# Ten chained stages on one core: the 96 conditioning pieces leave the first mixer, their sums and biases move to later chunks

## The chip, the cores and the metric

The kernel runs on one core of a Trainium2 chip. The metric is the device time in microseconds of one execution; lower is better. Each figure is a median of several runs, and one further execution was recorded by the hardware profiler. In what follows TensorE is also PE, VectorE DVE, ScalarE ACT, GpSimd POOL, and SyncE SP.

## The reference, cut to what matters

One sequence of 512 tokens with 1024 channels goes through two models in turn. The first has two layers, each a feed-forward block, a mixer and a second feed-forward block, with RMS norms; the second has two layers, each a hybrid mixer and a convolutional feed-forward block. Before each part of the second model a vector that depends only on the condition c scales and shifts the activations:

```python
cond = jax.nn.silu(c)
for l in range(DEPTH):
    mod = cond @ w_ada[l] + b_ada[l]                 # 1024 -> 6 * 1024, for each of two layers
    sh1, sc1, g1, sh2, sc2, g2 = [m[:, None, :] for m in jnp.split(mod, 6, axis=-1)]
    h = x * (1 + sc1) + sh1
    y = hybrid_mixer(h, ...)
    x = layer_norm(DN_ALPHA * x + g1 * y, ...)
    ...
```

So `mod` is twelve vectors of 1024 numbers (six for each layer). They are first needed when the second model starts; the kernel computes them meanwhile, in the shadow of the first model. This product is what the change moves.

## The kernel before, in words

**Stages and chunks.** All weights stream through the core once. They are cut into 522 chunks of eight 128x128 blocks (512 KB each). The ten stages use them in order: FFN1 (chunks 0 to 65), MIX0, the first mixer (66 to 95), FFN2 (96 to 161), FFN3 (162 to 227), MIX1 (228 to 259), FFN4, then the two hybrid mixers and the two convolutional blocks. `BASE` (L124) holds the first chunk of each stage. A chunk is loaded by SP into one of four RAW buffers, ACT copies its upper part to SPH (`halve_to`, L1541), and DVE makes the remainder SPL (`halve_to`, L2165 to L2177); PE then multiplies each block three times (L806 to L808: high with high, high with low, low with high). ACT and DVE work up to four chunks ahead of PE.

**Conditioning pieces.** Each of the 96 pieces `wa` (512 KB) takes a RAW buffer of its own, one after every two chunks, from chunk 2 to chunk 192. DVE adds c times the piece to ADA (`ada`, L2149 and L2152). Eight pieces make one of the twelve vectors. After the eighth, DVE transposes ADA (L2160) and reduces it to ADS (L2162, event `adas`). PE finishes the sum with eight tiny matmuls `adamm` at the start of a chunk c with c % 16 == 14 (`begin_chunk`, L782 to L790, event `adamm`), which is two chunks ahead of the place of the eighth piece in the order of the chunks. DVE adds the bias (`mods`, L2132 to L2136) when it comes to the first piece of the next vector (L2146 and L2147). The last piece comes with chunk 192.

**PSUM banks.** There are eight banks. Before anything is emitted, a planner walks through the program in PE's order and gives each result a bank (`Ring`, L158 to L184). Without a group it takes the next bank in turn; `ps.before(name)` is then the event after which that bank's former result has been read, and PE waits for it in front of the first matmul. `plan_chunk(c)` (L524 to L526) gives the `adamm` of chunk c a bank in the same turn. `plan_first` plans the six output tiles that the start of a stage (`project_first`) fills at once, then calls `plan_chunk` for the chunks of that stretch, and the stage then takes a bank for its sum of squares (`xsum`). The seventh tile, `("proj", s, 6)`, is planned after that. In a feed-forward stage DVE reads tile 0 as `gate` (L2294), tile 1 as `up` (L2297); in MIX1 it reads the tiles as `qk` (L2546), and there a small product `rcolp` (L1266) follows tile 6.

**The first mixer.** Its projection runs over 22 tiles (`project`, three matmuls for each of eight blocks), and DVE and ACT prepare what the recurrence needs in `prep(j, q)`, at the tiles listed in `PREP_AT`. DVE reads each tile with L2386 or L2389. PE takes part with small products: L1008 and L1010, L1014 (`kqmm`, which waits for ACT's `kq`, L1703), and L1023. Behind the projection an order written out by hand (`MIX0_TENSOR`, `MIX0_VECTOR`, ...) sets the queue of each engine. In it each product of the mixer names its banks by number, so the first of them in a bank waits for whatever tile the planner's turn has left there; the first is `("01", "lt", 1)`. The first four output tiles stand in banks 7, 5, 3 and 2. The remaining four go in turn again (`plan_out`). DVE copies output tile m out of its bank at L2229 (event `("y", s, m)`), after a square by ACT (L1602, L1605).

Of the kernel before, what the change touches and what calls it, by code (L numbers as in the profile page):

```python
# [17 lines left out]
NRAW = 4  # L18
NSPL = 4
ADA_EVERY = 3  # L20
N_ADA = 96
# [99 lines left out]
FFN1, MIX0, FFN2, FFN3, MIX1, FFN4, HYB0, CONV0, HYB1, CONV1 = range(10)  # L121
NAMES = {FFN1: "l0_ffn1", FFN2: "l0_ffn2", FFN3: "l1_ffn1", FFN4: "l1_ffn2"}
CHUNKS = [66, 30, 66, 66, 32, 66, 32, 66, 32, 66]
BASE = [sum(CHUNKS[:s]) for s in range(10)]  # L124
# [181 lines left out]
def build(nc, a, order, known):  # L306

    ctx = ExitStack()
    with ctx:
# [19 lines left out]
        RAW, _ = place("RAW", NRAW * CH * 128)  # L329
# [55 lines left out]
        def pc(name, i=0, n=1):  # L385
            return PCT[:, PC[name] + i:PC[name] + i + n]

        def xt(k):
            return X[:, k * T:(k + 1) * T]
# [13 lines left out]
        IDENT, MEANM, BD = CST[:, 0:128], CST[:, 128:256], CST[:, 256:384]  # L403
        ONE, EPS6, EPS5, EPSG, DECAY = [SML[:, i:i + 1] for i in range(5)]

        def item_of(n):

            return n + min(n // 2, N_ADA)

        def item_of_ada(i):  # L410
            return 3 * i + 2

# [106 lines left out]
        ps = Ring([b for b in banks])  # L521
        scr = Ring([SCR[:, i * T:(i + 1) * T] for i in range(5)])

        def plan_chunk(c):  # L524
            if c % 16 == 14 and c < 2 * N_ADA:
                ps.plan(("adamm", c // 16), ("mod", c // 16))  # L526

        def plan_first(s, name, ended, n=6):
            for i in range(n):
# [248 lines left out]
        def tensor_program(e):  # L778
            w = Waits(e, handles, known)
            tile = [0]  # L780

            def begin_chunk(c):  # L782
                w.wait_ge(("lo", c))
                if c % 16 == 14 and c < 2 * N_ADA:
                    b = c // 16
                    w.wait_ge(("adas", b), ("sel",), *ps.before("adamm", b))
                    for q in range(4):
                        mm = e.matmul(ps["adamm", b][32 * q:32 * q + 32, 0:8], SEL[:], ADS[:, q:32:4], start=True,
                                      stop=True, skip_group_check=True)
                    mm.then_inc(pe_done.did(("adamm", b)))  # L790
# [1337 lines left out]
        def vector_program(e):  # L2128
            w = Waits(e, handles, known)
            halved = [0]  # L2130

            def mods(b):  # L2132
                l, o = b // 6, b % 6
                w.wait_ge(("adamm", b))
                e.tensor_tensor(MOD[:, b * 8:b * 8 + 8], ps["adamm", b][:, 0:8], pc(f"b_ada_2{l}", 8 * o, 8),
                                ALU.add).then_inc(dve_done.did(("mod", b)))  # L2136

            def ada(i):

                b, k = i // 8, i % 8  # L2140
                c = pc("c_2", k)
                r = item_of_ada(i) % NRAW * 1024
                raw = RAW[:, r:r + 1024]
                w.wait_ge(("raw", item_of_ada(i)))
                if k == 0:
                    if b:  # L2146
                        mods(b - 1)  # L2147
                    w.wait_ge(("cond",))
                    e.tensor_scalar(ADA[:], raw, c, None, ALU.mult).then_inc(dve_done.did(("ada", i)))  # L2149
                else:  # L2150
                    w.wait_ge(("ada", i - 1))
                    e.scalar_tensor_tensor(ADA[:], raw, c, ADA[:], ALU.mult, ALU.add).then_inc(  # L2152
                        dve_done.did(("ada", i)))
                if i == 6:
                    w.wait_ge(("cst",))
                    e.tensor_reduce(SEL[:], IDENT.rearrange("p (a r) -> p r a", a=4), AX, ALU.add).then_inc(
                        dve_done.did(("sel",)))
                if k == 7:
                    w.wait_ge(("ada", i))
                    e.transpose(raw, ADA[:]).then_inc(dve_done.did(("adat", b)))  # L2160
                    w.wait_ge(("adat", b), *([("adamm", b - 1)] if b else []))
                    e.tensor_reduce(ADS[:], raw.rearrange("p (b c) -> p b c", c=32), AX, ALU.add).then_inc(  # L2162
                        dve_done.did(("adas", b)))

            def halve_to(c):  # L2165

                while halved[0] <= min(c, a["chunks"] - 1):
                    n = halved[0]
                    if n % 2 == 0 and 0 < n <= 2 * N_ADA:
                        ada(n // 2 - 1)  # L2170
                    if n == 2 * N_ADA + 2:
                        mods(N_ADA // 8 - 1)
                    w.wait_ge(("hi", n))
                    q, r = n % NSPL * 1024, item_of(n) % NRAW * 1024
                    e.tensor_tensor(SPL[:, q:q + 1024], RAW[:, r:r + 1024], SPH[:, q:q + 1024].bitcast(F32),  # L2175
                                    ALU.subtract).then_inc(lo_ready.did(("lo", n)))
                    halved[0] += 1  # L2177
# [906 lines left out]

        def sync_program(e):
            w = Waits(e, handles, known)
            items = [0]

            def load_to(j):

                while items[0] <= j:
                    i = items[0]
                    is_ada = i % 3 == 2 and i // 3 < N_ADA
                    n = i // 3 if is_ada else i - min((i + 1) // 3, N_ADA)
                    items[0] += 1
                    if not is_ada and n >= a["chunks"]:
                        continue
                    if i >= NRAW:
                        f = i - NRAW
                        if f % 3 == 2 and f // 3 < N_ADA:  # L3100
                            w.wait_ge(("adas", f // 24) if f // 3 % 8 == 7 else ("ada", f // 3))
                        else:
                            w.wait_ge(("lo", f - min((f + 1) // 3, N_ADA)))
                    r = i % NRAW
                    e.dma_start(RAW[:, r * 1024:(r + 1) * 1024], a["wa"][n] if is_ada else a["ws"][n]).then_inc(
                        landing(raw_landed[r], ("raw", i)), 16)

            def ahead(s):

                load_to(item_of(BASE[s] + AHEAD) + NRAW - 1)  # L3110

            e.dma_start(PCT[:], a["pc"]).then_inc(landing(pc_landed, ("pc",)), 16)
            for k in range(8):
                e.dma_start(xt(k), a["x"][:, k * T:(k + 1) * T]).then_inc(landing(x_landed[k], ("x", 0, k)), 16)
                if k < 3:
                    load_to(k)
            e.dma_start(CST[:], consts(["ident", "mean", "bd"])).then_inc(landing(cst_landed, ("cst",)), 16)
            for s in range(a["last"] + 1):
                if s == MIX0:
                    ahead(s)  # L3120
                    w.wait_ge(*ah_free(s))
                    e.dma_start(wk(41, 3), a["sm1"]).then_inc(landing(table_landed, ("sm1",)), 16)
                    w.wait_ge(("sm1",))
                    e.dma_start(rwkv["LV"], consts(["incl", "strict", "block", "first", "join2", "join4", "join8", "join16", "diag"])).then_inc(
                        landing(table_landed, ("lv",)), 16)
                elif s == MIX1:
                    ahead(s)
                    w.wait_ge(*ah_free(s), ("lv",))
                    e.dma_start(wk(24)[:, 0:384], consts(["suffix", "ones", "later"])).then_inc(
                        landing(table_landed, ("sufl",)), 16)  # L3130
                elif s in (HYB0, HYB1):
                    ahead(s)
                    H = hyb_places(s)
                    w.wait_ge(*ah_free(s), ("sufl",) if s == HYB0 else ("tables2", HYB0))
                    e.dma_start(WK[:, 23 * T:23 * T + NSM2], a["sm2"][(s - HYB0) // 2]).then_inc(
                        landing(table_landed, ("sm2", s)), 16)
                    w.wait_ge(("sm2", s))
                    e.dma_start(H["C1"][:, 0:3328], consts(["perm", "causal", "cos", "sin", "dec0", "dec1", "dec2",
                                                            "dec3"])).then_inc(
                        landing(table_landed, ("tables1", s)), 16)  # L3140
                    w.wait_ge(("tables1", s))
                    e.dma_start(H["C1"][:, 3328:3584], consts(["cmpm", "cmpn"])).then_inc(
                        landing(table_landed, ("tables2", s)), 16)
            load_to(a["chunks"] + N_ADA - 1)
            for k in range(8):
                w.wait_ge(("x", a["last"] + 1, k))
                e.dma_start(a["out"][:, k * T:(k + 1) * T], xt(k)).then_inc(landing(out_landed, ("out_dma", k)), 16)
            w.wait_ge(("out_dma", 7))
# [141 lines left out]
```

## Time and profile before

| | us |
|---|---|
| median of 3 runs (lowest, highest) | 3435.99 (3434.78, 3438.05) |
| the profiled execution, its own time | 3433.62 |
| its span, from first to last instruction | 3431.9 |
| PE busy (share of the span) | 3349.1 (98%) |
| PE weight loads busy | 2701.2 (79%) |
| DVE busy | 1980.5 (58%) |
| ACT busy | 1354.4 (39%) |
| mean granted clock of PE, as a share of full speed | 0.993 |

Busy times are sums of the records; matmuls overlap in them, so a busy PE isn't PE at its peak. A wait that is put down to a line means that the engine sat idle in front of an instruction until that line's instruction had ended.

### The profile page before, as it was taken

The page shows a single profiled execution, that of the slowest core. Times are in us where ns is not written, and L with a number is a line of the kernel's source. Part 1 is how long each engine was busy: PE and PEld are TensorE (multiplying, and loading weights), DVE is VectorE, ACT ScalarE, POOL GpSimd, SP SyncE. Part 2 cuts the span into 40 slices and gives each one's busy share as a digit, 9 for nine tenths or more (in the row PEclk, how much of TensorE's full clock was granted, in tenths as well). Part 3 has the DMA queues.
Part 4 walks back from the last instruction along what each step waited for, and adds up shares of the span by engine and source line. Part 5 has one row for each costly group of instructions (what it writes and reads, how often), then busy time and mean ns, then how long its engine had stood idle before and what let it go on. Part 6 is the DMA issues. An engine that isn't in the chain of part 4 may idle for free.

```text
span 3431.9 us, 43947 instructions
## 1 busy us (share of the span) xinstructions
PE 3349.1 (98%) x18588; PEld 2701.2 (79%) x18588; DVE 1980.5 (58%) x2869; ACT 1354.4 (39%) x2048; POOL 30.2 (1%) x68
## 2 busy tenths in 40 slices
PE   8999999999999999999999999999999999999998
PEld 6888868788888888886688888757888877578887
DVE  6554687675546653435464435586665365766644
ACT  4332466443324332326443323364443233644433
POOL 0000003000000000000000000000000000000000
PEclk9999999999999999999999999999999999999999
DMA  5444330244443433230122334101322241023231
GB/s 191 146 147 145 127 117 3 89 134 147 146 143 117 161 109 99 89 99 31 38 93 98 99 98 147 56 32 57 103 98 98 80 147 62 14 80 98 94 103 56
DMA packets 93076, 342.28 MB, mean 100 GB/s; under 512 B 10320, under 2 KB 10832, under 8 KB 92368
## 3 DMA queue, kind: packets, MB, share of 16 engines
q1 hardware_dynamic: 92880, 339.48, 30.3%
q8 instruction: 146, 2.39, 0.3%
q14 instruction: 50, 0.41, 0.0%
HBM read 337.34 MB, written 2.10 MB: 99 GB/s over the span
## 4 chain that ended last, share of the span: by engine, by line
PE 86%; DVE 7%; ACT 5%; issue 1%; POOL 0%; DMA 0%; SPq 0%; DVEq 0%; ACTq 0%; POOLq 0%
PE ps L806 21%; PE ps L808 20%; PE ps L807 20%; PE ps L874 3%; PE ps L875 3%; PE ps L878 2%; PE ps L921 1%; PE ps L923 1%; PE ps L922 1%; ACT WK L2069 1%; DVE SPL L2175 1%; PE ps L1296 1%; PE ps L897 1%; PE ps L898 1%; PE ps L899 1%; ACT SPH L1541 1%
## 5 line engine op out<-in xcount | busy, mean ns | idle before, releaser
L2175 DVE TENSOR_TENSOR SPL<-RAW,SPH 128x1024 fp32r<-128x1024 f32 x522 | 635.8, 1224 | 933.2 <-ACT SPH L1541 933.1
L1541 ACT ACTIVATE SPH<-RAW 128x1024 fp32r<-128x1024 f32 x522 | 547.9, 1056 | 976.6 <-PE ps L808 869.8
L806 PE MATMUL ps<-HH,SPH 128*128 128x512 f32 x2328 | 920.2, 395 | 9.2 <-DVE SCR L2294 4.6
L808 PE MATMUL ps<-HH,SPL 128*128 128x512 f32 x2328 | 908.6, 390 | 0.0
L807 PE MATMUL ps<-HL,SPH 128*128 128x512 f32 x2328 | 908.6, 390 | 0.0
L806 PEld LDWEIGHTS ps<-HH,SPH 128*128 128x128 f32 x2328 | 438.1, 188 | 113.5 <-issue 11.1
L807 PEld LDWEIGHTS ps<-HL,SPH 128*128 128x128 f32 x2328 | 438.1, 188 | 94.0 <-issue 4.3
L808 PEld LDWEIGHTS ps<-HH,SPL 128*128 128x128 f32 x2328 | 438.0, 188 | 91.4
L806 PE MATMUL ps<-AH,SPH 128*128 128x512 f32 x996 | 389.4, 391 | 2.7 <-DVE AH L2524 2.7
L808 PE MATMUL ps<-AH,SPL 128*128 128x512 f32 x996 | 388.0, 390 | 0.0
L807 PE MATMUL ps<-AL,SPH 128*128 128x512 f32 x924 | 360.0, 390 | 0.0
L806 PEld LDWEIGHTS ps<-AH,SPH 128*128 128x128 f32 x996 | 187.0, 188 | 43.0 <-DVE AH L2524 3.1
L808 PEld LDWEIGHTS ps<-AH,SPL 128*128 128x128 f32 x996 | 187.0, 188 | 38.9
L807 PEld LDWEIGHTS ps<-AL,SPH 128*128 128x128 f32 x924 | 173.5, 188 | 36.2 <-issue 0.5
L874 PE MATMUL ps<-HH,SPH 128*128 128x512 f32 x390 | 154.1, 395 | 10.7 <-DVE SPL L2175 10.2
L875 PE MATMUL ps<-HH,SPL 128*128 128x512 f32 x390 | 153.5, 394 | 0.0
L1676 ACT ACTIVATE SCR<-SCR 128x512 f32<-128x512 f32 x88 | 55.7, 633 | 170.8 <-DVE SCR L2294 170.8
L2152 DVE SCALAR_TENSOR_TENSOR ADA<-RAW,PCT,ADA 128x1024 f32<-128x1024 f32 x84 | 107.4, 1279 | 0.0
L878 PE MATMUL ps<-HL,SPH 128*128 128x512 f32 x408 | 104.4, 392 | 0.8 <-DVE HL L2208 0.8
L2722 DVE SCALAR_TENSOR_TENSOR SCR<-ps,PCT,SCR 128x511 f32<-128x511 f32 x88 | 65.7, 747 | 63.8 <-ACT SCR L1981 63.8
L2302 DVE TENSOR_TENSOR AL<-SCR,AH 128x512 fp32r<-128x512 f32 x88 | 61.0, 693 | 61.4 <-ACT AH L1678 61.4
L874 PEld LDWEIGHTS ps<-HH,SPH 128*128 128x128 f32 x390 | 74.0, 190 | 28.1 <-issue 9.9
(559 smaller groups left out, 4219.4 us busy)
## 6 DMA issues: line engine op xcount, KB each, us to landing
RAW<-in_ws SPq DMA_DIRECT2D x522, 512.0 KB, 3.3
RAW<-in_wa SPq DMA_DIRECT2D x96, 512.0 KB, 3.5
WK<-in_sm SPq DMA_DIRECT2D x2, 2784.0 KB, 10.6
WK<-in_cst SPq DMA_DIRECT2D x2, 1664.0 KB, 7.1
X<-in_x SPq DMA_DIRECT2D x8, 256.0 KB, 8.3
out<-X SPq DMA_DIRECT2D x8, 256.0 KB, 2.1
WK<-in_sm SPq DMA_DIRECT2D x1, 768.0 KB, 4.8
PCT<-in_pc SPq DMA_DIRECT2D x1, 349.0 KB, 2.9
```

The source lines that it names most:

```text
L806: e.matmul(out, wh, rhs[0], start=start, stop=False)
L807: e.matmul(out, wh, rhs[1], start=False, stop=False)
L808: mm = e.matmul(out, wl, rhs[0], start=False, stop=stop)
L874: e.matmul(ps["proj", s, i][:], wh, hh, start=k == 0, stop=False, skip_group_check=True)
L875: e.matmul(ps["proj", s, i][:], wl, hh, start=False, stop=False, skip_group_check=True)
L878: mm = e.matmul(ps["proj", s, i][:], wh, hl, start=False, stop=k == 7, skip_group_check=True)
L1541: e.activation(SPH[:, q:q + 1024], RAW[:, r:r + 1024], ACT.Copy).then_inc(hi_ready.did(("hi", n)))
L1676: e.activation(scr["g", s, m], scr["g", s, m], ACT.Silu).then_inc(act_done.did(("silu", s, m)))
L2152: e.scalar_tensor_tensor(ADA[:], raw, c, ADA[:], ALU.mult, ALU.add).then_inc(dve_done.did(("ada", i)))
L2175: e.tensor_tensor(SPL[:, q:q + 1024], RAW[:, r:r + 1024], SPH[:, q:q + 1024].bitcast(F32), ALU.subtract).then_inc(lo_ready.did(("lo", n)))
L2302: e.tensor_tensor(al(m), g, ah(m).bitcast(F32), ALU.subtract).then_inc(dve_done.did(("al", s, m)))
L2722: e.scalar_tensor_tensor(g[:, 1:T], b[:, 0:T - 1], pc(cwn, 44 + mt), g[:, 1:T], ALU.mult, ALU.add).then_inc(dve_done.did(("c1", s, i)))
```

## The change

The change has three parts and touches no arithmetic. First, `turn_of(n)` numbers the chunks without those of MIX0: no piece stands among chunks 66 to 95, and the pieces that stood there and all behind them come 30 chunks later, so that the last comes with chunk 222 (in FFN3). The order of loads is now a list, `items`, from which SP, ACT and DVE take their places. Second, the `adamm` products get places of their own: chunk 16 b + 17 instead of 16 b + 14, plus 30 for those at or past chunk 66; one that would fall into the last eight chunks before MIX0, FFN3 or MIX1 goes to the fifth chunk of FFN2, FFN3 or MIX1 instead. That makes chunks 17, 33, 49, 100, 111, 127, 143, 166, 175, 191, 207 and 232. Third, `mods(b)` runs when DVE comes to the chunk five behind its `adamm`, and no longer in front of the next vector's first piece.

```diff
--- before.py
+++ after.py
@@ -403,12 +403,34 @@
         IDENT, MEANM, BD = CST[:, 0:128], CST[:, 128:256], CST[:, 256:384]
         ONE, EPS6, EPS5, EPSG, DECAY = [SML[:, i:i + 1] for i in range(5)]
 
+        def turn_of(n):
+            if BASE[MIX0] <= n < BASE[FFN2]:
+                return None
+            return n - CHUNKS[MIX0] if n >= BASE[FFN2] else n
+
+        sums_at, mods_at = {}, {}
+        for b in range(N_ADA // 8):
+            n = 16 * b + 17
+            n += CHUNKS[MIX0] if n >= BASE[MIX0] else 0
+            for begin, after in ((MIX0, FFN2), (FFN3, FFN3), (MIX1, MIX1)):
+                if BASE[begin] - 8 <= n < BASE[begin]:
+                    n = BASE[after] + 4
+            sums_at[n], mods_at[n + 5] = b, b
+
+        items = []
+        for n in range(a["chunks"]):
+            v = turn_of(n)
+            if v is not None and v % 2 == 0 and 0 < v <= 2 * N_ADA:
+                items.append(("wa", v // 2 - 1))
+            items.append(("ws", n))
+        items = items[:a["chunks"] + N_ADA]
+        places = {item: i for i, item in enumerate(items)}
+
         def item_of(n):
-
-            return n + min(n // 2, N_ADA)
+            return places["ws", n]
 
         def item_of_ada(i):
-            return 3 * i + 2
+            return places["wa", i]
 
 
 
@@ -522,8 +544,9 @@
         scr = Ring([SCR[:, i * T:(i + 1) * T] for i in range(5)])
 
         def plan_chunk(c):
-            if c % 16 == 14 and c < 2 * N_ADA:
-                ps.plan(("adamm", c // 16), ("mod", c // 16))
+            b = sums_at.get(c)
+            if b is not None:
+                ps.plan(("adamm", b), ("mod", b))
 
         def plan_first(s, name, ended, n=6):
             for i in range(n):
@@ -781,8 +804,8 @@
 
             def begin_chunk(c):
                 w.wait_ge(("lo", c))
-                if c % 16 == 14 and c < 2 * N_ADA:
-                    b = c // 16
+                b = sums_at.get(c)
+                if b is not None:
                     w.wait_ge(("adas", b), ("sel",), *ps.before("adamm", b))
                     for q in range(4):
                         mm = e.matmul(ps["adamm", b][32 * q:32 * q + 32, 0:8], SEL[:], ADS[:, q:32:4], start=True,
@@ -2143,8 +2166,6 @@
                 raw = RAW[:, r:r + 1024]
                 w.wait_ge(("raw", item_of_ada(i)))
                 if k == 0:
-                    if b:
-                        mods(b - 1)
                     w.wait_ge(("cond",))
                     e.tensor_scalar(ADA[:], raw, c, None, ALU.mult).then_inc(dve_done.did(("ada", i)))
                 else:
@@ -2166,10 +2187,11 @@
 
                 while halved[0] <= min(c, a["chunks"] - 1):
                     n = halved[0]
-                    if n % 2 == 0 and 0 < n <= 2 * N_ADA:
-                        ada(n // 2 - 1)
-                    if n == 2 * N_ADA + 2:
-                        mods(N_ADA // 8 - 1)
+                    v = turn_of(n)
+                    if v is not None and v % 2 == 0 and 0 < v <= 2 * N_ADA:
+                        ada(v // 2 - 1)
+                    if n in mods_at:
+                        mods(mods_at[n])
                     w.wait_ge(("hi", n))
                     q, r = n % NSPL * 1024, item_of(n) % NRAW * 1024
                     e.tensor_tensor(SPL[:, q:q + 1024], RAW[:, r:r + 1024], SPH[:, q:q + 1024].bitcast(F32),
@@ -3084,25 +3106,22 @@
 
         def sync_program(e):
             w = Waits(e, handles, known)
-            items = [0]
+            loaded = [0]
 
             def load_to(j):
 
-                while items[0] <= j:
-                    i = items[0]
-                    is_ada = i % 3 == 2 and i // 3 < N_ADA
-                    n = i // 3 if is_ada else i - min((i + 1) // 3, N_ADA)
-                    items[0] += 1
-                    if not is_ada and n >= a["chunks"]:
-                        continue
+                while loaded[0] <= min(j, len(items) - 1):
+                    i = loaded[0]
+                    what, n = items[i]
+                    loaded[0] += 1
                     if i >= NRAW:
-                        f = i - NRAW
-                        if f % 3 == 2 and f // 3 < N_ADA:
-                            w.wait_ge(("adas", f // 24) if f // 3 % 8 == 7 else ("ada", f // 3))
+                        former, m = items[i - NRAW]
+                        if former == "wa":
+                            w.wait_ge(("adas", m // 8) if m % 8 == 7 else ("ada", m))
                         else:
-                            w.wait_ge(("lo", f - min((f + 1) // 3, N_ADA)))
+                            w.wait_ge(("lo", m))
                     r = i % NRAW
-                    e.dma_start(RAW[:, r * 1024:(r + 1) * 1024], a["wa"][n] if is_ada else a["ws"][n]).then_inc(
+                    e.dma_start(RAW[:, r * 1024:(r + 1) * 1024], a[what][n]).then_inc(
                         landing(raw_landed[r], ("raw", i)), 16)
 
             def ahead(s):
```

## Rows read from the trace of the kernel before

**Rows 1.** Part 1 of the page: busy time of each engine.

```profile
PE 3349.1 (98%) x18588; PEld 2701.2 (79%) x18588; DVE 1980.5 (58%) x2869; ACT 1354.4 (39%) x2048; POOL 30.2 (1%) x68
```

**Rows 2.** Stretches (mixer, late FFN3): us, busy per engine, clock, DMA share, GB/s.

```profile
370.00:610.00 240.00, 226.31 (x2621) 184.87 (x2621) 183.19 (x295) 145.44 (x233) 28.26 (x55) 0.96 0.23 74
1225.00:1425.00 200.00, 200.00 (x937) 167.99 (x936) 73.71 (x83) 54.65 (x63) 0.00 (x0) 1.00 0.29 95
```

**Rows 3.** Waits of PE, whole span: us in total, times, longest.

```profile
PE ps L860 <- ACT HH L1644: 7.3, 3, 2.7
...
PE ps L806 <- DVE SCR L2294: 4.6, 3, 2.4
PE ps L788 <- DVE ADS L2162: 4.0, 3, 2.4
```

**Rows 4.** Timeline, PE, mixer's projection: start, us, line, [idle before <-releaser].

```profile
420.71 0.50 PE L806 MATMUL ps<-HH,SPH 128*128 128x512 f32 x1 [1.53 <-DVE SCR L2386]
...
439.93 1.12 PE L1014 MATMUL ps<-WK,CST 128*128 128x512 f32 x2 [1.31 <-ACT WK L1703]
...
455.42 0.25 PE L788 MATMUL ps<-ADS,SEL 128*32 128x8 f32 x8 [2.41 <-DVE ADS L2162]
...
466.96 2.07 PE L1014 MATMUL ps<-SCR,CST 128*128 128x512 f32 x2 [3.17 <-ACT SCR L1703]
...
490.32 1.12 PE L1014 MATMUL ps<-WK,CST 128*128 128x512 f32 x2 [0.87 <-ACT WK L1703]
```

**Rows 5.** Timeline, DVE, the same stretch.

```profile
417.63 1.28 DVE L2152 SCALAR_TENSOR_TENSOR ADA<-RAW,PCT,ADA 128x1024 f32<-128x1024 f32 x1
...
442.17 1.23 DVE L2175 TENSOR_TENSOR SPL<-RAW,SPH 128x1024 fp32r<-128x1024 f32 x1 [2.96 <-ACT SPH L1541]
...
451.46 1.28 DVE L2152 SCALAR_TENSOR_TENSOR ADA<-RAW,PCT,ADA 128x1024 f32<-128x1024 f32 x1
...
455.19 1.22 DVE L2175 TENSOR_TENSOR SPL<-RAW,SPH 128x1024 fp32r<-128x1024 f32 x1
```

**Rows 6.** Timeline, PE, start of FFN2, tiles 6 and 7.

```profile
729.37 0.80 PE L806 MATMUL ps<-HH,SPH 128*128 128x512 f32 x1
...
736.51 0.50 PE L806 MATMUL ps<-HH,SPH 128*128 128x512 f32 x1 [1.10 <-DVE SCR L2294]
```

**Rows 7.** Timeline, DVE, FFN2, its reading of tile 0.

```profile
735.78 0.68 DVE L2294 TENSOR_TENSOR SCR<-ps,RS 128x512 f32<-128x512 f32 x1
```

**Rows 8.** Timeline, PE, start of FFN3, tile 7.

```profile
1102.60 0.50 PE L806 MATMUL ps<-HH,SPH 128*128 128x512 f32 x1 [1.10 <-DVE SCR L2294]
```

**Rows 9.** Timeline, PE, start of MIX1, tile 6 and rcolp.

```profile
1461.95 0.80 PE L806 MATMUL ps<-HH,SPH 128*128 128x512 f32 x1
...
1467.90 1.05 PE L1266 MATMUL ps<-CST,ACC 128*128 128x1 f32 x8
```

**Rows 10.** Timeline, DVE, MIX1, its reading of tile 0 and on.

```profile
1467.16 3.08 DVE L2546 SCALAR_TENSOR_TENSOR WK<-ps,RS 128x512 f32<-128x512 f32 x5
```

**Rows 11.** Timeline, PE, mixer's output, first of tile 0 and of tile 4.

```profile
658.40 0.50 PE L806 MATMUL ps<-AH,SPH 128*128 128x512 f32 x1 [2.69 <-DVE AH L2524]
...
669.41 0.39 PE L806 MATMUL ps<-AH,SPH 128*128 128x512 f32 x1
```

**Rows 12.** Timeline, DVE, its copy of the mixer's output tile 3.

```profile
672.51 0.68 DVE L2229 COPY WK<-ps 128x512 f32<-128x512 f32 x1
```

**Rows 13.** Timeline, DVE, end of the mixer's projection, bonus(3).

```profile
528.08 0.69 DVE L2336 TENSOR_TENSOR WK<-ps,WK 128x512 f32<-128x512 f32 x1
```

**Rows 14.** Stretches behind four stalls, columns as in Rows 2.

```profile
455.00:460.00 5.00, 4.58 (x20) 3.70 (x21) 4.08 (x7) 2.43 (x4) 0.00 (x0) 0.66 0.60 206
466.00:474.00 8.00, 7.04 (x17) 4.92 (x18) 5.54 (x10) 4.47 (x7) 0.00 (x0) 0.57 0.41 131
2748.00:2754.00 6.00, 5.72 (x30) 5.45 (x31) 5.93 (x15) 5.24 (x8) 0.00 (x0) 0.72 0.00 0
...
54.00:60.00 6.00, 5.78 (x25) 4.80 (x26) 4.39 (x8) 2.91 (x5) 0.00 (x0) 1.00 0.52 181
```

## The prediction, made before the changed kernel was run

> **What bounds the kernel now.** Read the busy times first: PE holds 98% of the span, DVE 58% [rows 1]. So a microsecond counts only where PE gets or loses it. The windows by stretch then show where PE isn't full: the mixer has 226.3 us of PE in 240 at a granted clock of 0.96, while the later part of FFN3 is full, with DVE busy for 73.7 of 200 us [rows 2]. Next the waits of PE, of which the longest are 2 to 3 us; the one on ADS is the direct target here, 4.0 us in three places [rows 3]. Last the timelines of PE and DVE around each long wait, and around each place where the change touches a bank. The reader is to see there that DVE and ACT, not PE, set the pace of the mixer's projection from tile 7 on [rows 4, 5], and that at the starts of FFN2, FFN3 and MIX1 the seventh tile is what PE works on while DVE comes to the first [rows 6 to 10].
>
> **Part 1, the pieces out of the mixer.** Ten of them lie between the start of the mixer's stage and the end of its projection. One takes 1.28 us of DVE, about 1.2 from start to start; the eighth of a vector, with its transpose and reduction, takes 3.7 (455.19 less 451.46) [rows 5]. What each gives back depends on what the next DVE instruction waits for:
> - the one at 417.63 stands in front of the reading that PE awaits at 420.71: 1.2 of the 1.53 us go [rows 4, 5];
> - another of its kind is in the chain to PE's wait at 439.93: 1.2 more of 1.31. The one behind it ends in DVE's own idle time of 2.96 us, for ACT, and gives nothing [rows 4, 5];
> - the block at 451.46 goes whole. DVE and ACT come 3.7 us earlier to kq, for which PE waits at 466.96. PE does not wait at 455.42 any more, but reaches kqmm earlier by as much and waits longer there, so the gain is not 2.41 + 3.17 but what the chain gains: 6.1 in all by 466.96 [rows 4, 5];
> - the next in the chain takes away the rest, 0.87, of the wait at 490.32 [rows 4]: 7.0.
>
> Behind that DVE waits for PE, and the pieces by the mixer's output lie in idle time. The adamm waits on ADS outside 455.42 go too, since their places now lie behind the vector's last piece: 4.0 less 2.41 is 1.6 [rows 3, 4]. Part 1 with these is worth 8.6 us. Bounds: 2 (only the waits of 420.71 and 490.32 shrink) to 12 (all five rows of rows 4, 9.3, with 1.6 and some of the clock). The pieces turn up in FFN3, where DVE has 126 of 200 us free and PE waits for nothing; fifteen at 1.28 are 19 us, so they cost nothing [rows 2, 5]. The number of loads, of adamm and of mods stays; SP, with four RAW buffers as before, is one load in three freer in the mixer. I put no time on that.
>
> **Part 2, the places of the sums, and the banks.** An adamm takes a bank in the planner's turn, so a moved one changes who has which bank. I walked the planner's turn through for both placements. Most of the changed results wait for something older or long read. Four places don't.
>
> First, FFN2. Chunk 100 is in the stretch that `plan_first` plans. Before, the banks went to six tiles, xsum, tile 6: eight, and tile 6 found the bank of the last stage's root. Now they go to six tiles, adamm 3, xsum: eight, and tile 6 gets the bank of tile 0, which DVE must have read. PE began tile 6 at 729.37 and had just run out of it when DVE read tile 0 at 735.78; it began tile 7 at 736.51 after 1.10 us of waiting [rows 6, 7]. Nothing that DVE does there hangs on tile 6 (it waits for the sum of squares, ACT's root and the halving ahead). So PE will stand still for 7.1 us and begin tile 6 where it began tile 7: a tile lost. 48 matmuls of the mixer's output take 11.01 us (669.41 less 658.40), so a tile's 24 take 5.5 [rows 11].
>
> Second, FFN3, chunk 166: the same, with the same 1.10 us in front of tile 7 at 1102.60 [rows 8]: 5.5.
>
> Third, MIX1, chunk 232. Tile 6 began at 1461.95, and rcolp followed at 1467.90, just when DVE had read tile 0 (1467.16 and one of five readings in 3.08 us) [rows 9, 10]. Now tile 6 waits for that reading: PE stands for 5.9 us, and rcolp comes a tile later, 5.5.
>
> Fourth, the mixer. There are two adamm less in its turn (chunks 78 and 94) and one less before it. The turn meets the numbered banks otherwise: output tile 4, which had bank 4, gets bank 2, and that is the bank of output tile 3, which PE has just finished. DVE copies that tile at 672.51 for 0.68 us [rows 12]; tile 4 began at 669.41 [rows 11]. So PE waits until 673.2: 3.8 us. Likewise the first numbered product, lt 1, comes to a bank of bonus(3), which DVE reads at 528.08 for 0.69 us, some 0.7 behind where PE began [rows 13]: 0.7.
>
> Sum of the waits: 3 x 5.5 + 3.8 + 0.7 = 21.0 us. Bounds 15 (a reading that comes earlier by a piece or so at each stage) to 22.
>
> **The clock behind the waits.** No row of before has a stall of PE of 4 to 7 us behind its start. The nearest: behind the stall of 2.41 us the granted clock averages 0.66 over 5 us, behind that of 3.17 it is 0.57 over 8, behind one of 2.7 it is 0.72 over 6, and behind one of 2.4 at the first feed-forward block it is 1.00 [rows 3, 4, 14]. Time lost is the stretch by one less the clock: 1.7, 3.4, 1.7 and 0. All of the four new stalls of 3.8 to 7.1 us are longer than the longest of these, so I take it that the clock falls to 1.2 GHz in each, and the middle of 1.7 and 3.4, 2.6, for each: 10.4. Bounds 0 and 13.7. The Trainium skill (TensorE: Matmul & The Clock Gate, section on the HAM clock gate) says that half rate is the array's default and that only activity releases it, so that each long idle gap is paid for a second time. By that rule all four stalls are followed by half rate; the trace agrees for three of the four that it shows. Without the rule I would give the rival without a clock loss twice its chance.
>
> **Part 3, the bias.** mods takes two small operands and none of its waits is late: its adamm is issued one chunk before DVE, four ahead, comes to it. In front of it in DVE's queue is nothing that PE awaits sooner than before. Zero, at worst some tenths.
>
> **Sum.** 21.0 + 10.4 - 8.6 = 22.8 us. The profiled execution took 3433.6 (span 3431.9) and would take 3456.4. The median of the runs is 2.4 above it, so the forecast for the median is 3458.8, slower by 0.66%.
>
> **Rivals.**
> - The clock stays up, or falls behind stalls too late to matter: 21.0 - 8.6 = 12.4, 3448. For it: the stall of 2.4 us with a clock of 1.00 [rows 14]. Against it: the other three, and the length of the new stalls. 0.10.
> - Faster: the bank waits don't bind, because by the time PE is at tile 6 DVE has read tile 0. This decides at one point, the 6 to 7 us between PE's start on tile 6 and DVE's reading [rows 6, 7, 9, 10]. If those readings came earlier by that much, only the gains are left: 3436.0 - 8.6 = 3427. Against it: they hang on a chain from PE's own xsum through ACT and three instructions of DVE, none of which the change takes away. For it: only that my walk through the planner could be wrong, though it explains each of the waits on L2294 and L2386 of before. 0.07.
> - Nothing to measure: the mixer gains all of its bound, 12, and the stalls cost the low end, 15, with a clock loss of 2 or less. 3441. 0.05.
> - Worse: the mixer gives back 2 only, since the wait for kq just grows, and every stall costs 3.4 of clock: 21.0 + 13.7 - 2 = 32.7, 3469. 0.10.
> - The forecast, 3459: 0.68.
>
> **How the numbers follow.** 0.2% is 6.9 us, about what these runs can tell from no change. Faster by more than that is the second rival: 0.07. Within it is the third and the edges of the others: 0.06. Slower is the rest: 0.87. The forecast's own range is 3450 to 3467; to hold eight in ten with the first rival and most of the last it goes from 3445 to 3468.
>
> **What would show it.** In the changed profile PE's longest waits should be three of 5.9 to 7.1 us in front of L806, released by L2294 (twice) and L2546, and one near 3.8 us released by L2229, each followed by a stretch at about half clock. The wait on ADS should be gone. The wait at the second kqmm (L1014) should be longer, near 3.7, and yet stand 6 us earlier. If the waits in front of tile 6 are there but last under 4 us, my reading that DVE hangs on xsum is wrong; if they are absent, the walk through the banks is. If PE's projection in the mixer ends at the same time as before, part 1 is wrong.

## The result, and the profile after

| | us |
|---|---|
| changed kernel, median of 4 runs (lowest, highest) | 3458.56 (3454.31, 3474.46) |
| kernel before, 4 runs on the same chip | 3435.59 (3434.78, 3438.05) |
| ratio, with its 95% interval | 1.0074 (1.0041 to 1.0107) |
| profiled execution of the changed kernel | 3456.04, span 3454.3, mean granted clock 0.990 |

Slower by 0.74%, where 0.66% was forecast; the profiled execution took 3456.04 us, and the sum had given 3456.4. So near a hit needs a look at the terms: two of them were wrong, in opposite directions.

In what follows the lines of the changed kernel stand 22 or 23 further down than before: L806 is now L829, L1014 L1037, L2294 L2316, L2229 L2251, L2546 L2568, L1541 L1564.

The page's busy times (against [rows 1]) are nearly the same. PE has 3.2 us more, which fits its lower mean clock (0.990 against 0.993).

```profile
PE 3352.3 (97%) x18588; PEld 2703.6 (78%) x18588; DVE 1981.0 (57%) x2869; ACT 1356.2 (39%) x2048; POOL 30.9 (1%) x68
```

The two stretches of [rows 2] show the load that was moved. DVE has 11.5 us less to do in the mixer and 26.7 more in late FFN3, and PE stays full there, as said.

```profile
370.00:610.00 240.00, 227.26 (x2644) 185.93 (x2644) 171.71 (x286) 147.28 (x235) 28.55 (x55) 0.96 0.16 52
...
1225.00:1425.00 200.00, 200.00 (x897) 165.08 (x896) 100.36 (x110) 54.34 (x62) 0.00 (x0) 1.00 0.44 141
```

Among the longest waits of PE over the whole span (total, times, longest) the ones on L2316, L2568 and L2251 are new. ADS is gone from the list; the one on HH is that of before [rows 3], and the one of 10.9 stands at the start of the program.

```profile
PE ps L829 <- DVE SCR L2316: 15.5, 3, 6.6
PE ps L897 <- DVE SPL L2197: 10.9, 2, 10.6
PE ps L883 <- ACT HH L1667: 7.3, 3, 2.7
...
PE ps L829 <- DVE WK L2568: 5.4, 1, 5.4
PE ps L1037 <- ACT SCR L1726: 5.2, 1, 5.2
PE ps L829 <- DVE WK L2251: 3.7, 1, 3.7
...
PE ps L1083 <- DVE WK L2358: 0.9, 1, 0.9
```

Where they stand is in PE's timeline: two answer to [rows 4], then output tile 4 [rows 11], the last matmul ahead of tile 6 of FFN2 with tiles 6 and 7 [rows 6], tile 6 of FFN3 [rows 8] and of MIX1 [rows 9].

```profile
420.06 0.50 PE L829 MATMUL ps<-HH,SPH 128*128 128x512 f32 x1 [0.33 <-DVE SCR L2408]
...
464.70 2.07 PE L1037 MATMUL ps<-SCR,CST 128*128 128x512 f32 x2 [5.16 <-ACT SCR L1726]
...
670.87 0.50 PE L829 MATMUL ps<-AH,SPH 128*128 128x512 f32 x1 [3.67 <-DVE WK L2251]
...
731.13 1.02 PE L929 MATMUL ps<-ACC,CST 128*128 128x512 f32 x2
738.73 0.79 PE L829 MATMUL ps<-HH,SPH 128*128 128x512 f32 x1 [6.58 <-DVE SCR L2316]
...
746.67 0.39 PE L829 MATMUL ps<-HH,SPH 128*128 128x512 f32 x1
...
1112.59 0.80 PE L829 MATMUL ps<-HH,SPH 128*128 128x512 f32 x1 [6.58 <-DVE SCR L2316]
...
1484.44 0.79 PE L829 MATMUL ps<-HH,SPH 128*128 128x512 f32 x1 [5.38 <-DVE WK L2568]
```

PE stands in front of such a line until DVE has read the bank. The bracket counts from the end of the record before; a matmul that waits for nothing begins before that end, so what the stall costs is a little more, as the ledger shows. In FFN2 tile 7, which waited 1.10 us before, now waits for nothing: the stall has only moved a tile ahead.

**The ledger.** Apart from the moved sums both traces hold the same matmuls in the same order, so each can be matched with its partner. The difference of the two starts, after less before, is the delay at that place. Its steps say what each place costs:

| stretch (time in the trace of before) | delay, from and to | step | forecast |
|---|---|---|---|
| up to the mixer's projection (413) | 0 to 0.55 | +0.55 | 0 |
| projection, up to behind 490.32 | 0.55 to -3.37 | -3.92 | -7.0 |
| rest of the mixer, with lt 1, to its output | -3.37 to -2.38 | +0.99 | +0.7 |
| stall of output tile 4 (669.41) | -2.38 to 1.46 | +3.84 | +3.8 |
| low clock behind it | 1.46 to 3.20 | +1.74 | +2.6 |
| to the sum of squares of FFN2 (728.91) | 3.20 to 2.22 | -0.98 | 0 |
| FFN2, from there to behind tile 6 | 2.22 to 10.16 | +7.94 | +8.1 |
| FFN3, the same stretch | 10.00 to 17.12 | +7.12 | +8.1 |
| chunk 174 (1131.28), its wait on ADS | 17.12 to 15.46 | -1.66 | -1.6 |
| MIX1, from the sum of squares to behind tile 6 | 16.55 to 23.64 | +7.09 | +8.1 |
| stretches between (-0.2 and +1.1), and all behind MIX1's start (-1.2, to 22.4) | | -0.3 | 0 |
| sum | | +22.4 | +22.8 |

In the three starts the delay jumps at tile 6 by 7.14 (2.22 to 9.36), 7.14 (10.00 to 17.14) and 5.94 (16.55 to 22.49), and grows within tile 6, at the low clock, by 2.05, 1.21 and 1.15; what tile 7 no longer waits goes off again in FFN2 and FFN3.

**The clock.** Granted clock (the column before the last two) behind the stalls of FFN2, FFN3, MIX1, output tile 4 and the mixer's kq:

```profile
739.00:745.00 6.00, 6.00 (x17) 4.74 (x18) 4.32 (x8) 3.11 (x5) 0.00 (x0) 0.60 0.41 161
1113.00:1119.00 6.00, 6.00 (x21) 4.76 (x21) 4.21 (x9) 3.05 (x5) 0.00 (x0) 0.76 0.45 154
1485.00:1491.00 6.00, 6.00 (x22) 4.79 (x21) 1.85 (x4) 0.00 (x0) 0.00 (x0) 0.75 0.32 113
671.00:679.00 8.00, 8.00 (x29) 6.39 (x30) 0.11 (x1) 0.74 (x2) 0.00 (x0) 0.79 0.16 58
...
464.70:472.70 8.00, 8.00 (x21) 5.69 (x22) 5.69 (x9) 4.46 (x6) 0.00 (x0) 0.62 0.20 66
```

It was low behind all four new stalls. Each stretch times one less its clock gives 2.4, 1.4, 1.5 and 1.7 us, 7.0 in all, and the ledger 2.05, 1.21, 1.15 and 1.74, 6.2 in all. The forecast was 10.4.

When the clock fell matters as much as that it fell. At the three starts it was down while PE still stood (in MIX1 0.52 from 1481 to 1484). At output tile 4 PE went on at 670.87, and the clock was still 0.99 up to 672.20. The rows are the last 1.7 us in which PE stood in FFN2, the last 3.5 in FFN3, and tile 4 from 672.20:

```profile
737.00:738.70 1.70, 0.00 (x0) 0.00 (x0) 1.70 (x3) 0.00 (x0) 0.00 (x0) 0.51 0.88 292
...
1109.00:1112.50 3.50, 0.00 (x0) 0.00 (x0) 3.50 (x5) 1.57 (x2) 0.00 (x0) 0.51 0.54 150
...
672.20:676.00 3.80, 3.80 (x11) 2.94 (x10) 0.00 (x0) 0.00 (x0) 0.00 (x0) 0.56 0.05 20
```

So a part of each low stretch at the starts lay in time that PE spent waiting, and cost nothing.

**The mixer's chain.** DVE and ACT at the place of the block that went, to be read against 455.19 in [rows 5]:

```profile
450.25 0.16 DVE L2380 COPY WK<-SCR 128x4 f32<-128x4 f32 x1
452.92 1.23 DVE L2197 TENSOR_TENSOR SPL<-RAW,SPH 128x1024 fp32r<-128x1024 f32 x1 [2.51 <-ACT SPH L1564]
```

```profile
448.83 1.28 ACT L1568 ACT_TABLE_LOAD   x1 [1.64 <-DVE WK L2370]
450.13 0.63 ACT L1736 ACTIVATE WK<-WK 128x512 f32<-128x512 f32 x1
...
451.84 1.04 ACT L1564 ACTIVATE SPH<-RAW 128x1024 fp32r<-128x1024 f32 x1
```

DVE is free at 450.41 and could make the remainder, but ACT's copy of the same chunk stands behind a table load and three activations and begins at 451.84. The kernel before has that copy here:

```profile
452.97 1.04 ACT L1541 ACTIVATE SPH<-RAW 128x1024 fp32r<-128x1024 f32 x1
```

There it was done 1.2 us ahead of DVE, which had the block of 3.7 us to do. ACT comes only 1.13 us earlier, by as much as PE was ahead already (delay -1.13 at 440). So SPL, DVE's remainder of the chunk, begins 2.27 us earlier, of which 1.14 is new. The delay gains as much there (1.12, from -1.13 to -2.25), and that is all that the block gives.

### The profile page after: what moved, and what is told of

Read it like the earlier page. It is cut to its first block, busy times and chain, and to the rows that moved or that the text cites. A ratio compares the mean times of both kernels' runs of the same rounds, so it can differ in the third digit from the quotient of the medians.

```text
span 3454.3 us, 43961 instructions
## 1 busy us (share of the span) xinstructions
PE 3352.3 (97%) x18588; PEld 2703.6 (78%) x18588; DVE 1981.0 (57%) x2869; ACT 1356.2 (39%) x2048; POOL 30.9 (1%) x68
## 4 chain that ended last, share of the span: by engine, by line
PE 89%; DVE 6%; ACT 4%; issue 1%; DMA 0%; POOL 0%; SPq 0%; DVEq 0%; ACTq 0%; POOLq 0%
PE ps L829 21%; PE ps L831 21%; PE ps L830 21%; PE ps L897 3%; PE ps L898 2%; PE ps L901 2%; PE ps L946 1%; PE ps L945 1%; PE ps L944 1%; ACT WK L2092 1%; PE ps L1319 1%; DVE SPL L2197 1%; PE ps L920 1%; PE ps L922 1%; PE ps L921 1%; ACT SPH L1564 1%
## 5 line engine op out<-in xcount | busy, mean ns | idle before, releaser
L829 PE MATMUL ps<-HH,SPH 128*128 128x512 f32 x2328 | 921.0, 396 | 25.0 <-DVE SCR L2316 15.5
L1564 ACT ACTIVATE SPH<-RAW 128x1024 fp32r<-128x1024 f32 x522 | 548.6, 1057 | 995.1 <-PE ps L831 888.9
L829 PEld LDWEIGHTS ps<-HH,SPH 128*128 128x128 f32 x2328 | 439.4, 189 | 131.6 <-DVE SCR L2316 17.9
L829 PE MATMUL ps<-AH,SPH 128*128 128x512 f32 x996 | 389.4, 391 | 6.4 <-DVE WK L2251 3.7
L829 PEld LDWEIGHTS ps<-AH,SPH 128*128 128x128 f32 x996 | 187.2, 188 | 47.4 <-DVE WK L2251 4.1
L897 PE MATMUL ps<-HH,SPH 128*128 128x512 f32 x390 | 153.6, 394 | 11.4 <-DVE SPL L2197 10.9
```

Of the source, the lines that this page charges most:

```text
L829: e.matmul(out, wh, rhs[0], start=start, stop=False)
L897: e.matmul(ps["proj", s, i][:], wh, hh, start=k == 0, stop=False, skip_group_check=True)
L1564: e.activation(SPH[:, q:q + 1024], RAW[:, r:r + 1024], ACT.Copy).then_inc(hi_ready.did(("hi", n)))
```

## The experiments

The changed kernel was timed once more, and six further kernels were made. e1, e2, e4 and e5 ran on one chip and e0, e3 and e6 on another, each beside the kernel before (medians 3437.76 and 3435.41), so runs of different groups are compared by their ratios. My theory: the banks' turn makes the new waits, and each is paid for where the trace shows it. The rival: the load in the other places (DVE with more pieces in FFN2 and FFN3, other loads) slows the stages, and the waits only show where PE gets to feel it. "Delay" is that of the ledger, always against the kernel before.

**The changed kernel once more (e0_after).** No edit.

> The changed kernel once more, beside the others on one chip, since its four runs lay between 3454 and 3474. Every theory: 3455 to 3460.

Measured: 3455.46 us (3453.04 to 3474.87), ratio 1.0067 (1.0050 to 1.0083). The waits are the same to 0.01 us; the clock behind the stalls of FFN2, FFN3 and MIX1:

```profile
740.00:746.00 6.00, 6.00 (x16) 4.70 (x17) 4.40 (x8) 3.11 (x5) 0.00 (x0) 0.57 0.45 171
1114.00:1120.00 6.00, 6.00 (x20) 4.83 (x21) 4.40 (x8) 3.12 (x5) 0.00 (x0) 0.73 0.50 170
1486.00:1492.00 6.00, 6.00 (x20) 4.76 (x21) 2.16 (x5) 0.00 (x0) 0.00 (x0) 0.72 0.41 132
```

The loss of 0.7% repeats, and so does the smaller clock term (2.6, 1.6 and 1.7 us for these three).

**The sums behind tile 6 (e1_starts).** The three sums at the starts of stages go from the fifth chunk to the eighth, so that they take their bank after tile 6. Their biases stay five chunks behind them.

```diff
-                    n = BASE[after] + 4
+                    n = BASE[after] + 7
```

> The changed kernel, with the three products of FFN2, FFN3 and MIX1 that stood in the fifth chunk moved to the eighth (chunks 103, 169, 235), behind tile 6 in the planner's turn. Theory (tile 6 waits for the reading of tile 0 because one product took a bank ahead of it): the three waits in front of tile 6 (6.58, 6.58 and 5.38 us) vanish, the 1.1 us in front of tile 7 come back, and the time falls by what these three places measured in the changed trace, 7.0 + 7.4 + 7.6 = 22 us, to 3436.6. Rival (the starts are slow because DVE is later there, with the pieces behind it): the waits move to tile 7, less than 5 us are gained, 3454 or more.

Measured: 3441.59 us (3437.46 to 3460.01), ratio 1.0021 (1.0007 to 1.0035). This takes away 0.53% of the 0.74%, about 18 us, where the theory had 22. PE's waits from the mixer to FFN2:

```profile
PE ps L1037 <- ACT SCR L1726: 5.2, 1, 5.2
PE ps L829 <- DVE WK L2251: 3.7, 1, 3.7
...
PE ps L811 <- DVE SCR L2319: 1.8, 1, 1.8
```

The wait in front of tile 6 is gone at all three starts, with the pieces and loads as in the changed kernel. What is left in FFN2 and FFN3 is a wait of the sum itself in front of tile 7, of 1.8 us instead of 1.10:

```profile
734.16 0.80 PE L829 MATMUL ps<-HH,SPH 128*128 128x512 f32 x1
...
741.99 0.25 PE L811 MATMUL ps<-ADS,SEL 128*32 128x8 f32 x8 [1.78 <-DVE SCR L2319]
```

The rival falls: it allowed less than 5 us. The place of the sum in the turn, and not the load, makes the three long stalls. What the theory had too high is in the trace. From the sum of squares of FFN2 (728.91) to behind tile 6 of MIX1 the delay grows by 4.3 us (4.79 to 9.07), against 21.4 in the changed kernel: 17.1 gained. In FFN2 and in FFN3 2.5 us each stay, of the wait of the sum with a low clock behind it (0.72 over 6 us), where the theory had only the old wait of 1.10 come back.

**The mixer's output moved on in the turn (e2_out4).** Two more steps of the turn ahead of the mixer's output, so that tile 4 meets another bank; the starts stay as in the changed kernel.

```diff
+            ps.at[ps.all] += 2
             plan_postnorm(s, BASE[s] + 22, 8)
```

> The changed kernel, with the planner's turn moved on by two banks in front of the mixer's output, so that output tile 4 stands in bank 4 again and waits for nothing of tile 3. Theory: the wait of 3.67 us on L2229 vanishes with the 1.7 us of low clock behind it: 5.5 us less, 3453. Rival (the clock was low for another reason): only 3.7 us less, 3455, with the granted clock behind the fourth tile still low. The three starts stay as they are.

Measured: 3454.16 us (3449.17 to 3471.04), ratio 1.0058 (1.0036 to 1.0079). The wait on L2251 is gone, those of 6.6, 6.6 and 5.4 stay. The ratio is 0.16% below the changed kernel's first measurement and 0.09% below its second, 5.5 and 3.1 us, with overlapping intervals: in direction as the 5.6 us of the ledger, but not shown by this pair of times. Between theory and rival the trace decides, for the theory: with no wait in front of tile 4 the clock behind it stays up, and the delay is 16.72 at tile 4 and still 16.72 at 680.06, where the changed kernel lost 3.84 and 1.74.

```profile
686.00:694.00 8.00, 8.00 (x37) 6.64 (x36) 4.03 (x6) 3.09 (x4) 0.00 (x0) 1.00 0.20 67
```

**Both (e3_both).** The two edits together.

> The changed kernel with both edits, the three products in the eighth chunk and the turn moved on by two in front of the mixer's output. Theory: the gains add, 22 + 5.5, 3431, and the wait of 0.88 us for the last bonus stays. Rival (the waits overlap with others, so that the second edit gives less once the first is made): 3434 or more.

Measured: 3434.60 us (3430.20 to 3450.39), ratio 1.0000 (0.9990 to 1.0009). Against e1 the ratio is lower by 0.21%, 7.2 us, and the two intervals overlap by 0.0002 only. Here tile 4 shows, if barely; its 5.6 us lie within what the pair allows. The time is the rival's ("3434 or more") and not the 3431 of the theory, but not for the rival's reason: the second edit gives no less behind the first. What is missing are the 4 us that e1 already gave too little. With the four long bank stalls gone, the change neither costs nor gives.

**The turn as it was before (e4_turn).** e1, and one step of the turn wherever the kernel before had a sum up to the mixer's end (chunks 62, 78 and 94), so that the mixer meets its old banks again.

```diff
             if b is not None:
                 ps.plan(("adamm", b), ("mod", b))
+            if c in (62, 78, 94):
+                ps.at[ps.all] += 1
```

> The changed kernel with the three products in the eighth chunk and the planner's turn moved on by one bank at chunks 62, 78 and 94, so that the mixer and its output meet the banks of the kernel before. Theory: 22 us less for the starts, 5.5 for output tile 4, and about 1 for the first numbered products, which waited 0.88 us for the last bonus: 3430, some 5.5 us faster than the kernel before. Rival (leaving the pieces out of the mixer is worth the full 8.6 us that was forecast and other costs hide it): 3427 or less.

Measured: 3431.61 us (3427.93 to 3445.89), ratio 0.9982 (0.9969 to 0.9996). PE's waits from the mixer to FFN2:

```profile
PE ps L1039 <- ACT SCR L1728: 5.2, 1, 5.2
PE ps L831 <- DVE AH L2548: 2.7, 1, 2.7
...
PE ps L813 <- DVE SCR L2321: 1.8, 1, 1.8
```

Output tile 4 and lt 1 wait for nothing. Without its bank stalls (but for the two of 1.8 us) the change gains 0.18%, 6 us. The matched matmuls have the projection 4.1 us ahead behind 490.32 (delay -0.91 to -5.02), as 3.9 in the changed kernel, and not 7.0. It is this that speaks against the rival; the time alone doesn't, since 3427 is 0.9974 and lies in the interval. That e4 stands 0.18%, 6 us, below e3, where about 1 was expected, isn't explained; the two intervals overlap by 0.0006.

**ACT one chunk ahead in the mixer (e5_act9).** e4, and ACT copies one chunk more before its part of `prep` at tile 9, ahead of the table load.

```diff
+                    elif i == 9:
+                        halve_to(BASE[s] + 14)
```

> As the run with the turn kept, but at tile 9 of the mixer ACT makes the upper part of chunk 80 in front of the root for kq, not behind it. Theory (the piece block of 3.7 us gave only 1.1, since DVE then waits 2.5 us for ACT's upper part, which stands behind the root, its table load and an exponential): DVE's wait of 2.51 us near 450 vanishes, kq comes 2.5 us earlier, PE's wait of 5.2 us shrinks to 2.7, and 2.5 us are gained, up to 4 if the clock then stays up: 3426 to 3427.5. Rival (the chain to kq hangs on DVE's own work): no gain, 3430.

Measured: 3429.49 us (3422.34 to 3431.42), ratio 0.9969 (0.9958 to 0.9980). DVE's idle time in front of the remainder is gone, and the second kqmm waits 3.67 us instead of 5.16:

```profile
451.24 1.22 DVE L2201 TENSOR_TENSOR SPL<-RAW,SPH 128x1024 fp32r<-128x1024 f32 x1
```

```profile
448.01 1.04 ACT L1566 ACTIVATE SPH<-RAW 128x1024 fp32r<-128x1024 f32 x1
449.75 1.28 ACT L1570 ACT_TABLE_LOAD   x1 [0.69 <-DVE WK L2374]
```

```profile
463.02 2.07 PE L1039 MATMUL ps<-SCR,CST 128*128 128x512 f32 x2 [3.67 <-ACT SCR L1728]
```

Over the projection the delay goes from 1.48 to -5.13, a gain of 6.6 us, next to the 7.0 that was forecast for the removal alone; the wait of 3.67 is the one that the prediction had named. The step at kq alone, from 440 to 468, is 3.72 us (-0.22 to -3.94), as much as the block takes; in e4 it was 1.13. So most of the missing 3 us were ACT's queue. The wait came out at 3.67 where 2.7 was expected, and the median at 3429.5 where the theory had at most 3427.5 and the rival 3430: the traces decide here, not the times. Whether ACT's earlier copy would give anything in the kernel before was not tried; there DVE waits for nothing at that place. This version beats the kernel before by 0.31%, about 10.6 us. That it beats e4 is not shown: the intervals overlap, and the profiled executions (3429.88 and 3428.95) differ by a start into the mixer that is 2.4 us later in e5, ahead of any edit.

**The sums and biases alone (e6_sums).** The kernel before with all its pieces where they were; only the sums stand three chunks on (those of vectors 3, 5 and 9 further, at chunks 73, 103 and 169) and the biases five behind them.

```diff
+            n = 16 * b + {3: 25, 5: 23, 9: 25}.get(b, 17)
+            sums_at[n], mods_at[n + 5] = b, b
```

> The kernel before with its pieces in the mixer as they were; only the products go three chunks further on (to chunks 17, 33, 49, 73, 81, 103, 113, 129, 145, 169, 177, 193, the ones that would meet the end or start of a stage to its eighth chunk) and the bias five behind them. Theory (in the mixer the wait on ADS only stood in front of the wait for kq, which hangs on DVE and ACT): the wait of 2.41 us at ADS becomes part of the wait for kq, and only the 1.6 us of the two other waits on ADS are gained: 3434. Rival (the wait on ADS and its low clock were a loss of their own): 2.4 + 1.7 + 1.6, 3430.

Measured: 3437.24 us (3428.84 to 3458.68), ratio 1.0011 (0.9995 to 1.0027). PE's waits from the mixer to FFN2:

```profile
PE ps L1020 <- ACT SCR L1709: 5.2, 1, 5.2
PE ps L812 <- DVE AH L2528: 2.7, 1, 2.7
PE ps L794 <- DVE SCR L2390: 2.2, 1, 2.2
...
PE ps L1020 <- ACT WK L1709: 2.0, 1, 2.0
```

The wait on ADS of 2.41 us is gone, and kqmm waits 5.2, not 3.17: the two have become one, as PE reaches kqmm earlier and kq comes when it did. The second kqmm begins where it began (delay -0.04). Behind the third, at 490.32, a low clock follows, and the delay is 1.5 at 500. The one of 2.2 is a moved sum in front of a tile, for a bank that DVE has still to read. The rival's 3430 (0.9983) lies outside the interval. The theory's 3434 lies at its edge: the 1.6 us that were expected don't show in the time, and the moved sums brought waits of their own: the 2.2 us, and 1.8 in FFN2 and FFN3. Taking away the wait that was the plainest in the mixer is worth nothing by itself.

## Why the prediction was right, and where it was not

**The walk through the banks: right.** Four waits were named, with line, releaser and size: PE to stand for 7.1, 7.1 and 5.9 us at the starts and 3.8 at output tile 4. The delay jumps by 7.14, 7.14, 5.94 and 3.84. e1 takes the three away by the place of three small products alone; e2 takes the fourth, and e4 the fourth and that of lt 1 (0.88 us, 0.7 forecast). That DVE's reading of tile 0 hangs on PE's own sum of squares holds to a hundredth: in FFN2 it begins at 737.99 against 735.78, 2.21 later, and the sum of squares was 2.22 late. Only "a tile lost", 5.5 for each start, was short: less the clock the starts cost 5.9 each, 1.2 more in all, with tile 4 and lt 1 1.4.

**The clock: right in kind, too dear by 4.** "The middle of 1.7 and 3.4, 2.6, for each" was the step that failed; it is 6.2 us for four. The stalls are longer than those of [rows 14], but what the low clock costs behind them is about the same: by windows the rows behind 2.41 and 2.7 us had 1.7 us each, and those behind the three of 5.4 to 6.6 have 1.4 to 2.4. The prediction didn't ask when in the stall the clock falls. At the starts it had fallen 1.7 to 3.5 us before PE went on, and that part was free. The 3.4 taken as the upper end came from the stall for kq, where in the kernel before the clock fell only 0.7 us before PE went on (at 466.96), so that nearly the whole low stretch was paid for:

```profile
466.20:466.90 0.70, 0.00 (x0) 0.00 (x0) 0.57 (x1) 0.70 (x3) 0.00 (x0) 0.50 0.00 0
```

What decides when within or behind a stall the clock falls, these runs don't show. The Trainium skill (TensorE: Matmul & The Clock Gate, the section on the HAM clock gate) says that the throttled state is the default and activity releases it. The traces agree for all four stalls, in both executions looked at: each is followed by low clock. But it doesn't tell the price, and shorter stalls went either way (below).

**The mixer's chain: wrong by 3 us.** The sign that the prediction had named, a wait near 3.7 at the second kqmm that stands 6 us earlier, did not come: it is 5.16, and kqmm begins 2.26 us earlier. The step that failed is "the block at 451.46 goes whole. DVE and ACT come 3.7 us earlier to kq". Of the terms 1.2, 1.2, 3.7 and 0.9 the matched matmuls have 1.2 (delay 0.55 to -0.65), 0.5 (to -1.13), 1.1 (to -2.25 at 468) and 1.1 (to -3.37). In the two that fell short DVE waits for ACT's copy instead of working on the piece: 0.60 us of idle time at 430.83 and 2.51 at 452.92.

```profile
430.83 1.23 DVE L2197 TENSOR_TENSOR SPL<-RAW,SPH 128x1024 fp32r<-128x1024 f32 x1 [0.60 <-ACT SPH L1564]
```

I had asked what DVE's next instruction waits for at one place (the idle 2.96 us at 442.17) and not at the others, since in the trace of before it waits for nothing there: the piece had covered ACT's lateness. e5 shows it from the other side, with 6.6 us once ACT is ahead.

**What cost nothing: right.** PE is as full in late FFN3 as before with 26.7 us more on DVE (19 were counted for the fifteen pieces), and no wait of the biases appears. The ADS waits outside gave 1.7 us, 1.6 said, all at chunk 174.

**Why the total hit.** 22.8, less 4.2 of clock, and with 3.1 less gain in the mixer, 1.4 more in the waits and 0.7 less in the rest, is 22.4. Two errors of 3 and 4 us, one in each direction, cancel, so that 3458.8 against 3458.56 is luck and not the quality of the working. Nor is the median that exact: the repeat gave 3455.46, and the interval of the ratio is 11 us wide to each side.

## What to carry to other kernels

Where buffers are handed out in turn, a tiny operation is as heavy as a large one: three sums of eight matmuls of 8 columns, standing three chunks too early, cost 18 us (e1), since a tile then got a bank before DVE had read it. Before moving anything in such a program, walk the turn for both placements and look at who has which bank at each tight place; after it, put the turn back (e4). And when work is taken from one of two engines that feed each other, the other's queue is the next wait: look for it in the instructions that now have nothing in front of them, and move it too (e5).

## What the runs showed of the hardware that was not expected

**The clock is not a function of the stall.** PE's stall of 2.38 us at the start of FFN1's output tiles is in both traces. Before, the 6 us behind it had a clock of 1.00 [rows 14]; in the changed kernel, with no part of the change ahead of it, it is this:

```profile
54.00:60.00 6.00, 6.00 (x21) 4.73 (x20) 4.14 (x8) 3.00 (x5) 0.00 (x0) 0.72 0.44 157
```

Likewise the stall of 1.78 us in front of FFN2's tile 7: in e1 the clock behind it is 0.72, in e4 1.00.

```profile
742.00:748.00 6.00, 6.00 (x27) 4.78 (x28) 4.25 (x7) 2.84 (x4) 0.00 (x0) 0.72 0.41 148
```

```profile
735.00:741.00 6.00, 6.00 (x27) 4.96 (x28) 4.24 (x7) 2.85 (x4) 0.00 (x0) 1.00 0.35 119
```

And behind the 2.69 us in front of the mixer's output tile 0, a stall that every trace has, the clock is 1.00 over 6 us in the traces of before and after and 0.72 in the other seven. So a single execution gives or takes 1.7 us at each such place, and a step of the ledger is no surer than that where the clock plays a part.

**A stretch of small matmuls can stay at half clock.** In the mixer, behind a stall of 2.4 us, the execution of e2 that was profiled ran 40 us at 0.52, with PE busy throughout in short matmuls:

```profile
540.00:580.00 40.00, 40.00 (x662) 36.66 (x660) 19.53 (x37) 20.18 (x27) 1.42 (x2) 0.52 0.01 2
```

The trace of the changed kernel with the same stall has 0.97 over the same stretch, that of the kernel before 0.94. The time is really lost there: the delay in e2 goes from -3.48 at 528 to 15.09 at 600, in the changed kernel from -2.49 to -2.38. That execution took 3469.85 us against a median of 3454.16, and the profiled one of e3 likewise (3449.82 against 3434.60). Single runs 12 to 22 us above their kernel's median are in the lists of seven of the eight changed kernels' measurements (the 3474.46 above is one), and in none of the 50 runs of the kernel before. That they all are this stretch is likely, and shown only for the two that were profiled. The Trainium skill (the same page and section) tells of a clock seen stuck low for 50 us and more, at a quarter; here it is half, over 40 and more. What sets it off stays open.
